# The first norm's sums of squares: additions on two vector engines, or one-column matmuls over each squared tile

## What is computed

```
x = x + 1/2 * SwiGLU_1(RMSNorm(x))
h = RMSNorm(x)
x = x + W_out( sigmoid(gate_r) * A(h) + sigmoid(gate_a) * B(h) )     A: retention, B: windowed attention
x = x + 1/2 * SwiGLU_2(RMSNorm(x))
y = RMSNorm(x)

rmsnorm(x, g) = x * rsqrt(mean(x*x) + EPS) * g
swiglu(x) = (silu(x @ w_g) * (x @ w_u)) @ w_out
```

## Time and profile before

| | |
|---|---|
| median of 3 runs | 2230.14 us (2228.70 to 2230.19) |
| span of the profiled execution, first to last instruction | 2228.3 us |
| what lies around the span (median less span) | 1.8 us |
| PE busy | 2195.8 us, 99% of the span |
| PEld, DVE, ACT, POOL busy | 80%, 29%, 24%, 30% |
| first matmul of the kernel | 11.38 us |
| first matmul of unit 2 | 45.21 us |

### The profile page before, as it was taken

How to read it: one execution, slowest core, us unless ns; L and a number is a source line. 1 busy time by engine, 2 the same in 40 slices (tenths; PEclk the granted TensorE clock), 3 DMA queues, 4 the chain that set the end, 5 groups by cost and what they waited for, 6 DMA issues and landing times.

```text
span 2228.3 us, 25077 instructions
## 1 busy us (share of the span) xinstructions
PE 2195.8 (99%) x9848; PEld 1789.8 (80%) x9848; DVE 647.6 (29%) x607; ACT 530.5 (24%) x646; POOL 670.8 (30%) x294
## 2 busy tenths in 40 slices
PE   7999999999999999999999999999999999999997
PEld 5888888888887888888876778888888888888875
DVE  5112111111114434543764555331111111111122
ACT  4112122310113221212144454222210111111221
POOL 5333223322335412221211112353332233323342
PEclk9999999999999999999999999999999999999998
DMA  3111111111113211112111124211111111111112
GB/s 131 57 47 47 47 48 47 47 57 47 47 47 119 81 59 53 47 57 75 58 47 48 38 102 143 104 66 47 47 47 48 47 47 56 48 47 47 47 57 85
DMA packets 37618, 135.72 MB, mean 61 GB/s; under 512 B 4432, under 2 KB 4560, under 8 KB 37584
## 3 DMA queue, kind: packets, MB, share of 16 engines
q1 hardware_dynamic: 30528, 111.16, 14.7%
q10 hardware_dynamic: 7056, 24.08, 2.9%
HBM read 118.45 MB, written 16.78 MB: 61 GB/s over the span
## 4 chain that ended last, share of the span: by engine, by line
PE 89%; issue 6%; POOL 2%; DVE 1%; ACT 1%; DMA 0%; DVEq 0%; POOLq 0%; ACTq 0%
PE ps L295 82%; PE ps L502 2%; POOL w_lo L1216 2%; PE ps L524 2%; PE ps L516 1%; DVE a_lo L905 1%; DVE x L1207 0%; PE ps L418 0%; PE ps L431 0%; PE ps L353 0%; PE ps L455 0%; PE ps L474 0%; DMA mat<-mats 0%; POOL gs L1231 0%; PE ps L465 0%
## 5 line engine op out<-in xcount | busy, mean ns | idle before, releaser
L1216 POOL TENSOR_TENSOR w_lo<-stage,w_hi 128x1024 fp32r<-128x1024 f32 x188 | 472.2, 2512 | 1063.4 <-ACT w_hi L612 1063.4
L295 PE MATMUL ps<-a_hi,w_hi 128*128 128x512 f32 x2112 | 673.6, 395 | 15.9 <-DVE a_lo L905 14.2
L295 PE MATMUL ps<-a_hi,w_lo 128*128 128x512 f32 x2112 | 662.1, 390 | 0.0
L295 PE MATMUL ps<-a_lo,w_hi 128*128 128x512 f32 x2112 | 662.0, 390 | 0.0
L295 PEld LDWEIGHTS ps<-a_hi,w_hi 128*128 128x128 f32 x2112 | 395.0, 188 | 100.6 <-issue 12.2
L295 PEld LDWEIGHTS ps<-a_hi,w_lo 128*128 128x128 f32 x2112 | 397.1, 188 | 83.2
L295 PEld LDWEIGHTS ps<-a_lo,w_hi 128*128 128x128 f32 x2112 | 397.3, 188 | 82.7
L612 ACT ACTIVATE w_hi<-stage 128x1024 fp32r<-128x1024 f32 x188 | 197.7, 1051 | 535.5 <-PE ps L295 479.4
L295 PE MATMUL ps<-b_hi,w_hi 128*128 128x512 f32 (+1 forms) x832 | 259.9, 393 | 0.5 <-POOL w_lo L1216 0.5
L295 PE MATMUL ps<-b_lo,w_hi 128*128 128x512 f32 (+1 forms) x832 | 256.4, 389 | 0.0
L295 PE MATMUL ps<-b_hi,w_lo 128*128 128x512 f32 (+1 forms) x832 | 256.2, 389 | 0.0
(11 more groups left out here) (166 smaller groups left out, 1102.5 us busy)
## 6 DMA issues: line engine op xcount, KB each, us to landing
stage<-wstream SPq DMA_DIRECT2D x188, 512.0 KB, 3.2
gate_in<-gate_spill ACTq DMA_DIRECT2D x16, 512.0 KB, 5.2
x<-xT SPq DMA_DIRECT2D x8, 512.0 KB, 9.4
x_spill<-x ACTq DMA_DIRECT2D x8, 512.0 KB, 2.6
gate_spill<-gs ACTq DMA_DIRECT2D x8, 512.0 KB, 2.6
gate_spill<-sg ACTq DMA_DIRECT2D x8, 512.0 KB, 2.6
x<-x_spill SPq DMA_DIRECT2D x8, 512.0 KB, 3.9
outT<-x SPq DMA_DIRECT2D x8, 512.0 KB, 3.1
```

What stands on the lines that cost most here:

```text
L295: mm = pe.matmul(ps[:, bank, :], w[0:r, parity, k, :], moving[0:r, k, HALF * half:HALF * half + HALF], start=first and part == 0, stop=fin ...
L1216: pool.tensor_tensor(w_lo[:, parity, :, :], stage[:, parity, :, :], f32(w_hi[:, parity, :, :]), ALU.subtract).then_inc(wlo_done, 1)
```

## The change

The squares are no longer added up tile by tile. PE takes each squared tile as it comes: `tile_sums(m)` makes eight one-column matmuls over `x_sq[m]`, one for each token chunk, into columns 8m to 8m+7 of PSUM bank 4. They stand in PE's order behind the `part` calls of tile m. VectorE then adds the eight tiles' columns in one reduction to `rinv`, which ScalarE's root reads in place of PSUM. POOL has no additions left in this norm; the clearing of `rstd` is gone. `spread(0)` moves from between the last two `part` calls to behind both. The other norms keep their additions; their semaphore counts are shifted by one.

```diff
                 for k in range(KT):
                     pe.wait_ge(alo_done, k + 1)
                     part(0, k)
                     if k >= 2:
                         part(1, k - 2)
-                sums(0)
+                    mm = tile_sums(k)
+                mm.then_inc(tiles_summed, 1)
                 part(1, KT - 2)
+                part(1, KT - 1)
                 spread(0)
-                part(1, KT - 1)
...
+                def tile_sums(m):
+                    pe.wait_ge(sq_done, m + 1)
+                    for t in range(CH):
+                        mm = pe.matmul(ps[:, 4, CH * m + t:CH * m + t + 1], x_sq[:, m, P * t:P * t + P], ones[:, 0:1],
+                                       start=True, stop=True)
+                    return mm
...
             def root(p):
-                if p < 3:
-                    act.wait_ge(sums_done, p + 1)
+                if p == 0:
+                    act.wait_ge(acc_done, KT)
+                    total = rinv[:, :]
+                elif p < 3:
+                    act.wait_ge(sums_done, p)
                     total = ps[:, 4, 0:CH]
...
-            dve.memset(rstd[:, :], 0.0).then_inc(acc_zero, 1)
             for m in range(KT):
                 a_low(0, m, m)
-                if m > POOL_SQ:
-                    dve.wait_ge(sq_done, m + 1)
-                    if m > POOL_SQ + 1:
-                        dve.wait_ge(tail_added, m - POOL_SQ - 1)
-                    dve.tensor_tensor(x_sq[:, POOL_SQ, :], x_sq[:, POOL_SQ, :], x_sq[:, m, :], ALU.add
-                                      ).then_inc(tail_added, 1)
-            dve.wait_ge(tail_added, KT - POOL_SQ - 1)
-            dve.wait_ge(acc_done, POOL_SQ)
-            dve.tensor_tensor(rstd[:, :], rstd[:, :], x_sq[:, POOL_SQ, :], ALU.add).then_inc(acc_done, KT - POOL_SQ)
+            dve.wait_ge(tiles_summed, 1)
+            dve.tensor_reduce(rinv[:, :], ps[:, 4, 0:KT * CH].rearrange("p (m t) -> p t m", t=CH), AX.X, ALU.add
+                              ).then_inc(acc_done, KT)
...
-            pool.wait_ge(acc_zero, 1)
-            for m in range(POOL_SQ):
-                pool.wait_ge(sq_done, m + 1)
-                if m > 0:
-                    pool.wait_ge(acc_done, m)
-                pool.tensor_tensor(rstd[:, :], rstd[:, :], x_sq[:, m, :], ALU.add).then_inc(acc_done, 1)
```

More of the change, by code:

```diff
@@ L38 @@
 BIG = -1e30
-POOL_SQ = 5
 SEED = 1
@@ L194, in block_program @@
         final_sum = sem("final_sum")
-        tail_added = sem("tail_added")
+        tiles_summed = sem("tiles_summed")
         sums_done, std_done, rinv_done = sem("sums_done"), sem("std_done"), sem("rinv_done")
@@ L889, in recip @@
                 if p == 3:
+                    dve.wait_ge(sums_done, p)
+                    dve.tensor_copy(rinv[:, :], ps[:, 4, 0:CH]).then_inc(final_sum, 1)
                     dve.wait_ge(sums_done, p + 1)
-                    dve.tensor_copy(rinv[:, :], ps[:, 4, 0:CH]).then_inc(final_sum, 1)
-                    dve.wait_ge(sums_done, p + 2)
                     dve.wait_ge(final_sum, 1)
@@ L1276, in _ @@
                 pool.sem_inc(s, 16 * SEED)
-            pool.wait_ge(acc_zero, 1)
-            for m in range(POOL_SQ):
-                pool.wait_ge(sq_done, m + 1)
-                if m > 0:
-                    pool.wait_ge(acc_done, m)
-                pool.tensor_tensor(rstd[:, :], rstd[:, :], x_sq[:, m, :], ALU.add).then_inc(acc_done, 1)
-            ffn(0, 0, 2, KT)
+            ffn(0, 0, 1, KT)
             with pool.Fori(0, RH) as h:
@@ L1323, in _ @@
                     split(2 * i + (U_MERGE + b + 1), (U_MERGE + b + 1) % 2)
-            pool.wait_ge(acc_zero, 3)
+            pool.wait_ge(acc_zero, 2)
             with pool.Fori(0, KT // 2) as i:
@@ L1329, in _ @@
                     accumulate(2 * i + (2 * KT + b), b)
-            ffn(U_FFN2, FB + 1, 4, 3 * KT)
+            ffn(U_FFN2, FB + 1, 3, 3 * KT)
 def _tables():
```

## The result

The changed kernel takes 2242.43 us (median of 4 runs, 2238.36 to 2246.53) against 2229.82 (2228.70 to 2230.19): ratio 1.0057, 95% interval 1.0043 to 1.0071. It is 12.6 us slower where 10.9 (2241.0 us) was forecast, and its runs lie 8 us apart where those of before lie within 1.5. The profiled execution is the longest of them, 2246.53 us with a span of 2244.4.

The account below looks back on a forecast made before the run. PE's queue of matmuls was taken to bound the kernel: -4.8 (waits) + 12.6 (groups) + 1.8 (one at the low clock) + 1.3 (spread last) = +10.9, giving 2241.0 us; range 2237.5 to 2246.5.

Parts of the forecast that it names:

- The bound and the waits: First norm's stage: PE is the only bound; its waits for `a_lo` go, -4.8 us, and relieving POOL and VectorE adds nothing.
- The price of a group: Behind each tile, eight one-column matmuls cost PE 1.8 us; seven more groups, +12.6 us, nothing hiding them.
- The rival with nearly free narrow matmuls: First norm: weight loads run under wide matmuls' streaming, so the change is not slower; at half break-even 2228.1 us; chance 0.04.
- break-even: Price of a narrow record at which the change would neither gain nor lose time: 0.036 us.
- the sum of 41.2: PE's queue up to unit 2 if narrow matmuls cost nothing: 41.2, 4.0 before now.
- Spread last: Ahead of unit 2: `spread(0)` behind both last `part` calls leaves PE idle longer, +1.3 us; the sum chain stays hidden.
- The clock: Start of first norm: clock rises after the same twelve wide matmuls, at 20.2, with one group at the low clock, +1.77 us.
- late clock: First norm: the clock rises only in tile 2's twelve wide matmuls, +15.1, 2245.2 us; chance 0.26 (+12 to +16).
- Moved: Step on `spread(0)` going behind both last `part` calls: 1.36 us more PE idleness less 0.1 for a restart, +1.3 us.
- Its own signs of being wrong: In the changed profile: groups' spacing not 0.106; expected were one long group, unit 2 at about 56, nothing different afterwards.
- beyond tile 1: Sign of being wrong: wide matmuls behind the narrow groups still spaced 0.43 us after tile 1.

Follow-up runs that it names:

- Half the groups: Changed kernel without the narrow groups of tiles 0, 2, 4 and 6, their squares missing from the sums: 2237.70 us.
- no additions: Kernel before with the additions left out on both engines, rstd becoming the square of tile 7 alone: 2227.67 us.
- groups late: Changed kernel with the narrow groups of tiles 0 and 1 moved behind tiles 2 and 3: 2244.06 us.
- additions on VectorE: Kernel before with all eight additions on VectorE, one behind each a_lo, and none on POOL: 2228.05 us.
- POOL adds too: Changed kernel with POOL's five additions into rstd back as work that nobody reads: 2243.73 us.
- repeated kernel: The changed kernel run and profiled once more, without any edit: median 2243.19 us, ratio 1.0062.
- control with the early matmuls: Kernel before with seven float32 matmuls on a constant tile ahead of PE's wait for the constants: 2229.73 us.
- the early matmuls: Changed kernel with seven never-read float32 matmuls on a constant tile ahead of PE's wait for the constants: 2241.55 us.
- the matmuls behind the wait: Changed kernel with six never-read float32 matmuls on a constant tile that began only when the last constant had landed: 2244.14 us.

## Why the prediction was right, by its own steps

- **The bound and the waits.** Right, and shown. PE waits for no `a_lo` behind the first, and with POOL's additions put back nothing changes.
- **The price of a group.** 1.86 us in place of 1.8: a tile with twelve wide matmuls and a group takes 4.57, twelve steady ones 2.71. At the low clock it is 3.27 to the next wide one, 0.204 a record and 1.57 more than at the high clock; the forecast took 1.77, since the 3.57 of the earlier trace rows runs to a modelled end and the 1.8 from start to start. Half the groups gave 6.5 us of the stage back. The rival with nearly free narrow matmuls is out; each group had its 1.70 us or more everywhere. Its break-even was slightly off: the sum of 41.2 holds none of the groups, so the 4.0 us are shared by all 128 records, 0.031 us each and not 0.036.
- **Spread last.** +1.3 forecast, 1.35 between the two profiles with equal clocks. The chain of reduce (0.23), root and reciprocal was hidden.
- **The clock.** The term that was mis-sized: "So I take the same twelve wide matmuls ..., with one group at the low clock: +1.77 us". Three profiles of the same PE order had it rise behind 18, 24 and 6 wide matmuls, with two, two and no groups at the low clock. For the first profile the surplus over the twelve is 2 x 1.57 + 1.2 = 4.3 where 1.8 was taken. What failed was to take one execution's twelve for a property of the kernel. Even with no narrow group ahead, the profiles have 6 wide matmuls at the low clock (no additions), 12 (before), 18 (groups late) and 19 (additions on VectorE); the rise comes 4 to 10.6 us behind the first of them. With groups ahead it is 6 (POOL adds too), 18, 23, 24 and 24, and the rise comes 2.7, 14.7, 14.7, 17.2 and 17.2 us behind the first. So the groups seem to put the rise off, but one profile of each kernel doesn't separate that from the spread. The median lies with the *late clock* rival rather than with the forecast; its +15.1 was above the measured 12.6 of the total, though not above the stage of the repeated kernel, +15.15. The Trainium skill ("TensorE: Matmul & The Clock Gate", section "What's actually happening") says that the warm-up is a budget of time and not of matmuls. In these traces neither the count of twelve nor the time of 18.7 held. The same section says that the moment varies from run to run because the chip's observation doesn't start with the kernel, and with that the scatter of 8 us agrees; the kernel before hides this variation under its waits, as its control with the early matmuls shows for an early rise.
- **Not foreseen.** The fall behind unit 2, 1.7 us, seen in the first profile, with the groups late, with POOL's additions, with the early matmuls, with half the groups and with the matmuls behind the wait: six of seven profiles with `spread` last, none of seven with a `part` behind it. It belongs to the step "Moved", which was priced at the 1.3 us of lost cover alone. It can't be told which of the runs without a profile have it.
- **Its own signs of being wrong.** Two of them came. Tile 2's first six wide matmuls ran at 0.43, "beyond tile 1" (23.77 to 26.48), and something was different afterwards, the fall behind unit 2. Two groups were long and not one, and unit 2 started at 59.63 and not at about 56. The mechanism stands (PE's queue, priced by groups), the clock's course in it didn't.

By its sum: -4.8 + 12.6 + 0.5 (groups at 1.86) + 1.3 + 4.3 makes 13.9 of the 13.97 us of the stage; the start (+0.45) and the fall (+1.7) make it 16.1, and that run, 2246.53, is just above the range's upper end. The profile of the repeated kernel is of its median run. There the stage is 15.15 longer than before, but the start was 0.8 earlier and the stretch behind unit 2 1.6 shorter (the last groups at the high clock), 12.8 us of span in all. Neither of the two is the change's work. So that the median came within 2 us of the forecast is in part luck. The range, 2237.5 to 2246.5, had room for a late clock for the right reason, and for the unforeseen fall only by chance.

## What to carry to other kernels

One-column matmuls with a new stationary operand each weren't cheap: 0.106 us a record at the high clock, the same as the 128-column records of `spread`, with the weight loads busy 1.98 us for a group's 16 (from 27.69 of the changed kernel). That the load is what they cost, and not some fixed price of a record, is read from these rows; no run keeps the operand or swaps the two. A sum over 128x1024 numbers made so cost 1.86 us on the engine that bounds the kernel, to free two engines that didn't. Idle time on the bounding engine hides other costs, here the low clock at the start; who fills that idleness with work pays them. And before work is moved off two engines, see whether it is their running side by side that makes it dear: eight additions on VectorE alone were quicker than three there and five on POOL.

## What the runs showed of the hardware

- The granted clock can fall while PE is busy without a gap. With 32 narrow records back to back from 27.75 (groups late) it was at 0.50 by 30.5; with 32 of them from 21.44 it had stayed at 1.00, and with single groups of 1.7 us and twelve wide matmuls between them it stayed there for 23 us.
- The moment of its rise is no constant of a kernel: 18 and 24 wide matmuls at the low clock in two profiles of the same program.
- `a_lo` (VectorE, two SBUF inputs) takes 1.28 us alone and 2.9 to 3.2 beside POOL's additions, and these take 3.3 each; on VectorE an addition of the same size takes 1.21.
- The clock column shows 1.00 at the start also where wide matmuls start 0.43 us apart (11 to 26.4 of the changed kernel); up to the first fall, the spacing is what tells.
